# RWKV's odd heads run in the same rounds as the even heads instead of five rounds behind

## The reference

```python
def wkv7_scan(r, w, k, v, a, bb):
    def step(S, inp):
        r_t, w_t, k_t, v_t, a_t, b_t = inp
        sa = jnp.einsum('bhvk,bhk->bhv', S, a_t)
        S = S * w_t[:, :, None, :] + sa[..., None] * b_t[:, :, None, :] + v_t[..., None] * k_t[:, :, None, :]
        return S, jnp.einsum('bhvk,bhk->bhv', S, r_t)
...
    y = wkv7_scan(rh, decay.reshape(b, s, H, N), kh, vh, -kk, kk * ah)
```

## Time and profile before

| | |
|---|---|
| median of 3 runs | 3024.86 us (3021.54 to 3025.31) |
| span of the profiled execution | 3025.1 us; the page gives no other time of its own |
| PE busy | 2901.6 us, 96% |
| DVE busy | 2112.8 us, 70% |
| ACT busy | 1564.3 us, 52% |
| POOL busy | 680.0 us, 22% |
| rounds in which heads run | 1283 to 1883 us of the span |

### The profile page before, as it was taken

One profiled execution on the slowest core, in us unless ns is written; L12 is line 12 of the kernel. 1 busy time (PEld: TensorE's weight loads), 2 busy tenths in 40 slices (PEclk: granted clock), 3 DMA queues, 4 the chain that ended last, 5 costly groups with the idle time before them and its releaser, 6 DMA issues.

```text
span 3025.1 us, 52413 instructions
## 1 busy us (share of the span) xinstructions
PE 2901.6 (96%) x21006; PEld 2597.7 (86%) x21006; DVE 2112.8 (70%) x3455; ACT 1564.3 (52%) x2611; POOL 680.0 (22%) x869
## 2 busy tenths in 40 slices
PE   8977999999999999899899999998999999999998
PEld 8867998888888888888788888997888888888887
DVE  7888877865778656677777776777666665566654
ACT  6445555543555545366555555555445444444443
POOL 0455311210111000565455540001000110011100
PEclk9888999999999999899999999999999999999999
DMA  6312555556555555322222223454555555655554
GB/s 255 130 42 94 172 176 188 194 170 194 206 184 193 167 176 207 112 99 95 88 92 92 92 92 113 153 182 152 176 173 183 193 190 171 209 188 189 186 173 143
DMA packets 79825, 475.34 MB, mean 157 GB/s; under 512 B 8224, under 2 KB 11296, under 8 KB 38304
## 3 DMA queue, kind: packets, MB, share of 16 engines
q1 hardware_dynamic: 76768, 459.66, 44.3%
q10 hardware_dynamic: 2816, 12.32, 1.2%
HBM read 465.66 MB, written 6.29 MB: 156 GB/s over the span
## 4 chain that ended last, share of the span: by engine, by line
PE 77%; DVE 10%; issue 6%; ACT 4%; POOL 2%; DMA 0%; SPq 0%; ACTq 0%; POOLq 0%; DVEq 0%
PE bank L720 33%; PE bank L724 22%; PE bank L722 6%; PE bank L723 5%; DVE m L1247 2%; PE bank L742 1%; ACT m L2177 1%; POOL m L2901 1%; PE bank L1046 1%; POOL m L2897 1%; DVE m L1572 1%; PE bank L1050 1%; PE bank L1157 0%; PE bank L1008 0%; PE bank L1015 0%
## 5 line engine op out<-in xcount | busy, mean ns | idle before, releaser
L724 PE MATMUL bank<-m,m 128*128 128x256 f32 x6864 | 1930.3, 281 | 0.0
L720 PE MATMUL bank<-m,m 128*128 128x512 f32 x4736 | 1657.1, 394 | 5.7 <-DVE m L2051 5.7
L1247 DVE TENSOR_TENSOR m<-m,m 128x1024 fp32r<-128x1024 f32 (+1 forms) x944 | 1072.5, 1144 | 613.2 <-ACT m L2177 606.9
L724 PEld LDWEIGHTS bank<-m,m 128*128 128x128 f32 x6864 | 1300.3, 189 | 0.9
L2177 ACT ACTIVATE m<-m 128x1024 fp32r<-128x1024 f32 (+1 forms) x944 | 911.6, 979 | 712.9 <-PE bank L724 689.2
L720 PEld LDWEIGHTS bank<-m,m 128*128 128x128 f32 x4736 | 890.8, 188 | 203.4 <-DVE m L2051 5.9
L722 PE MATMUL bank<-m,m 128*128 128x256 f32 x2128 | 637.3, 299 | 29.2 <-DVE m L1247 23.5
L723 PE MATMUL bank<-m,m 128*128 128x256 f32 x2128 | 604.7, 284 | 0.0
L722 PEld LDWEIGHTS bank<-m,m 128*128 128x128 f32 x2128 | 409.7, 193 | 53.5 <-issue 42.9
L723 PEld LDWEIGHTS bank<-m,m 128*128 128x128 f32 x2128 | 410.2, 193 | 1.9
L2877 POOL TENSOR_TENSOR m<-m,m 128x256 fp32r<-128x256 f32 x44 | 63.4, 1441 | 683.0 <-ACT m L2454 683.0
(11 more groups left out here) (382 smaller groups left out, 2892.4 us busy)
## 6 DMA issues: line engine op xcount, KB each, us to landing
m<-in_w_up SPq DMA_DIRECT2D x88, 1024.0 KB, 4.8
m<-in_w_down SPq DMA_DIRECT2D x128, 704.0 KB, 4.1
m<-in_w_gu SPq DMA_DIRECT2D x88, 1024.0 KB, 4.8
m<-in_w_out SPq DMA_DIRECT2D x48, 1024.0 KB, 5.1
m<-in_w_krv SPq DMA_DIRECT2D x48, 1024.0 KB, 4.8
m<-in_w_xbc SPq DMA_DIRECT2D x24, 1024.0 KB, 4.8
m<-in_w_z SPq DMA_DIRECT2D x16, 1024.0 KB, 4.8
m<-in_w_in SPq DMA_DIRECT2D x14, 1024.0 KB, 6.6
```

The lines of the kernel that those rows point to most:

```text
L720: pe.matmul(bank.rearrange("p (a b) -> p a b", a=2), hi, x, start=kc == L.k0, stop=False)
L724: m = pe.matmul(ps, lo, x[:, 0, :], start=False, stop=last)
L1247: v.tensor_tensor(lo_of(k), raw_of(k)[0], hi_of(k).bitcast(F32), SUB).then_inc(*lo_v(("lo", k)))
```

## The change

The odd heads' generator starts each pair in the same round as the even heads', not five rounds later. `tails` and `afters` keep their rounds, and no instruction is added or removed.

```diff
     def heads(e):
-        return timed(*((PAIRS + ROUNDS * b + 5 * e, chain(block(2 * b + e, 0), block(2 * b + e, 1))) for b in range(8)))
+        return timed(*((PAIRS + ROUNDS * b, chain(block(2 * b + e, 0), block(2 * b + e, 1))) for b in range(8)))
 
     tails = timed(*((PAIRS + ROUNDS * (i // 2 + 1) + 5 * (i % 2), tail(i)) for i in range(16)))
```

## The result

The changed kernel takes 3046.51 us, the median of 4 runs (3043.06 to 3049.17), against 3023.92 (3021.54 to 3025.31) for the kernel before on the same chip. The ratio is 1.0073, with a 95% interval of 1.006 to 1.0085: slower, as forecast, inside the range, but by 22.6 us instead of 32. The profiled spans give the same picture, 3043.9 against 3025.1 us, so 18.8 us more.

What follows compares the result with a forecast made beforehand. PE, busy 96% of the span, was taken as the bound, losing time where it waits. Steady cycles at 5.9 us gave 23.6, plus 5.3 and 3: 32 us on 3025.1, so 3057 us, range 3034 to 3074.

Steps and rivals of the forecast that it cites:

- What bounds it: PE, busy 96% of the span, loses time where it waits; ACT sets the end in rounds 9 to 13.
- What is free: No instruction added or removed; odd heads ending five rounds sooner saves nothing, as PE does those matmuls either way.
- Rounds 0 to 7 free for waits: No prep there; ACT's spreads and DVE's two L1879 are wanted later, so costed at nothing.
- Round 8: L950 waits for L1931 behind a second state copy, 0.75 us instead of 0.2: +0.55 a cycle.
- Rounds 9 to 13: ACT 2.5 us late at the weight cut, so L1015 waits 3.0 us for L1879 instead of 1.05: +1.95 a cycle.
- Cycle 0: Like a steady cycle but without tails: 5.9 - 0.55 = 5.3 us slower.
- Round 11: ACT 0.55 us late from two more copies, so PE waits at L1001 for L2547: +0.5 a cycle.
- The clock: One fall to 1.2 GHz a cycle, after L1015's wait of 3.0 us, lasting 6.8 us: +3.1 a cycle.
- Rounds 15 to 17: DVE some 3 us late: waits of 1.6 us in rounds 16 and 17 at full clock, none with a fall.
- Cycles 2, 6, 7: Cycle 2: +3 us, bounds 0 and 5.9; cycles 6 and 7: taken as 0, between -2 and +6.
- The rival "faster": In step, waits at L1046 in rounds 6 to 9 and 16 to 19 go: -10 us, 3015; chance 0.09.

Runs made afterwards that it cites:

- experiments 2: Changed kernel with ACT's spreads L2553 late, even head's at end of step 2, odd head's at end of step 3: 3030.06 us, ratio 1.0019 to the kernel before.
- experiment 5: Changed kernel with both heads' spreads late (ends of steps 2 and 3) and the odd tail one round earlier: 3026.65 us, ratio 1.0012 to the kernel before.
- experiment 9: Changed kernel with only the odd head's spread L2553 late, at the end of its step 3: 3036.05 us, ratio 1.0037 to the kernel before.
- experiment 1: Changed kernel, but on PE alone the odd head's step stands two steps of main behind the even head's: 3084.88 us, ratio 1.0201 to the kernel before.
- experiment 4: Changed kernel with the odd head's tail one round earlier: 3034.48 us, ratio 1.0037 to the kernel before.
- experiment 8: Changed kernel, late spreads everywhere, early odd tail for pairs 0 to 5, pairs 6 and 7 five rounds apart: 3025.01 us, ratio 1.0000 to the kernel before.
- experiment 7: Changed kernel with the odd heads one round behind the even heads, tails unchanged: 3034.03 us, ratio 1.0037 to the kernel before.
- experiment 3: Kernel before, odd heads still five rounds behind, with both heads' spreads late (ends of steps 2 and 3): 3026.15 us, ratio 1.0002 to the kernel before.

## Why the prediction was right in direction and too high

The account of cycle 4, from the windows: PE's idle time is 75.40 - 70.72 = 4.7 us against 1.5, **+3.2**; the fall costs **+1.4**; PE's own work is 70.72 - 1.4 = 69.3 against 71.77, **-2.4**. Sum +2.2, and 75.40 - 73.24 is 2.2. The forecast had +5.9.

- **What bounds it.** Right: time was lost where PE waits, and at the engine named, ACT, in rounds 9 to 13.
- **"What is free": "those matmuls are PE's either way". This is the step that failed.** The matmuls are the same and their cost isn't. In step, like stands beside like and PE changes form 16 times fewer in a cycle. Own work fell by 2.4 us in cycle 4, and by 1.9, 2.0 and 2.1 in experiments 2, 5 and 9, at full clock: 15 to 19 us over eight cycles, 0.12 to 0.15 us a change. The pages agree: PE's busy time fell by 8.1 us although the mean granted clock fell from 0.981 to 0.977, some 25 us more at the lower level; at the 0.41 us of cost for each us there (1.4 for 3.4) that is 10 us, so its own work fell by some 18 (an estimate). With that term the forecast of 32 us would have been 13 to 17, against 18.8 measured. That form is the cause rests on experiment 1: the split costs time only in rounds whose form differs from `main`'s. The Trainium skill has the rule ("TensorEngine Tiling (Array Packing)", Key Properties): changing the tiling mode drains the engine, which changing the tile alone doesn't. The trace agrees as to the cost, 0.12 to 0.18 us a change; the drain itself no run here shows. I had read the change only for what waits, not for what stands beside what on PE.
- **Rounds 0 to 7 free for waits.** Right: in cycles 1, 3, 4 and 5 the trace shows no wait of PE there.
- **Round 8.** L950's wait was put at 0.75 and is 0.84. Experiment 4 gained 11.4 us by moving the tail, of which L950's waits are 6.6; the rest came with fewer falls of the clock, and that the one caused the other isn't shown.
- **Rounds 9 to 13.** ACT's lateness was put at 2.5 us: L2177 starts 13.83 us after round 9 now and 11.70 before, 2.1. The missing 0.4 is a misreading of mine: ACT's work before was not one long run. It had a wait for DVE in it, in the part that the earlier trace rows leave out, and took up 0.43 us of its lateness there, as that wait is now 1.04 us and was 1.47. L1015's wait was put at 3.0 and is 3.36 to 3.46 in cycles 1, 3, 4 and 5. Both within 0.5 us, and experiment 9 confirms the chain nearly microsecond for microsecond (1.72 us out of ACT's run, 1.62 off the wait). Cycle 0, for which I had the same wait, has none, and had none before: the five waits in the earlier trace rows are those of cycles 1 to 5. ACT's wait inside its run, in the timeline of the kernel before:

```profile
1621.74 0.51 ACT L2470 ACTIVATE m<-m,m 128x256 f32<-128x256 f32 x1 [1.47 <-DVE m L1712]
```

- **Round 11.** The wait of 0.5 at L1001 didn't come in cycle 4. L2547 was to be 0.55 us late; it starts 6.53 us after round 9 now and 6.33 before, 0.2 later, as ACT's wait for DVE took up the rest here too.
- **The clock.** The fall came, in all four cycles, and was mis-sized: I had 6.8 us at the low level and 3.1 us of cost each. It was 6.8 long in cycles 1 and 5 and 3.4 in 3 and 4. The cost in cycle 4 is 1.4; in cycle 5 it is 2.9 (PE busy 72.13 us, and 69.26 in the cycle 5 of experiment 4, which has no fall). (Cycle 7 had a longer wait at L1001, 2.95 us for 1.91, and a longer low stretch than the earlier trace rows.) I had taken the length from one fall, in cycle 7. The price for each us at the low level was nearly right, 0.46 by the earlier trace rows and 0.41 to 0.42 measured, though what stands in it is L1015 and L932 and not `main` alone.
- **Rounds 15 to 17.** Right: with a fall 0.30 us is left; without, in experiment 9, 2.1 (forecast 1.6).
- **Cycles 2, 6, 7.** I had +3 for cycle 2 and it is +3.3; 0 for cycles 6 and 7, and they are +1.1 and, with all that follows, +2.1. Cycle 0 was put at 5.3 and is 1.8. That cycles 6 and 7 are near 0 is luck: PE's idle time grew by 3.3 us in cycle 6 (5.3 against 2.0) and by 4.9 from cycle 7 on (31.5 against 26.6), where L1001 waits 2.95 us for 1.91 and L1071 of the last tails 3.50 for 0.41, and PE's cheaper work paid for most of it.

Added up, the forecast had 13.5 us of new waits in cycles 0, 1, 3, 4 and 5, 15.5 of falls and 3 for cycle 2. Measured are 26.9 us of idle time, some 10 of falls and 18 less of PE's own work. So the time is inside the range partly by luck: waits that I didn't see and a saving that I didn't see stand against each other.

The rival "faster" had a true half, which its text didn't name. Its place, L1046 for L1900, was wrong: those waits went up, from 5.1 us to 8.3. But order does save PE time, by form, and had ACT had the 2.5 us free, the change would have been near even: experiment 5 has steady cycles of 72.4 us against 73.2.

What stays open: why the clock falls behind some waits and not behind others, and so why it fell less in experiment 4 and elsewhere in experiment 8; what would spare cycles 0 and 6 their longer waits in step. That no version was faster is shown only for those tried.

## What to carry to other kernels

When two like streams of work are put in step, follow the engine with the longest run of in-order work ahead of something that a third engine needs (here ACT's weight cut), and add to it all that both streams now issue in that run: this came out within 0.5 us. Look for waits inside the run, which take up part of what is added (0.4 us here). Then read the bound engine itself: count how often its neighbours in the order change form, before and after, since the same matmuls in another order don't cost the same. Take the cost of a fall of the clock from the matmuls that will stand in it, and its length from more than one fall.

## What the runs showed of the hardware that I had not expected

- PE pays for a change between matmuls of different weight form: about 0.18 us each by experiment 1 (4.9 us for 28), 0.2 by experiment 7 (1.5 us for 7), 0.12 to 0.15 by the comparison with before (1.9 to 2.4 us for 16). Round 9 of experiment 1 by itself gives 0.17. Between steps of the same form as `main` nothing was seen (2.76 and 2.75 us).
- The clock's fall behind a wait isn't certain by the wait's length alone. It stayed at 1.00 behind 1.74 us in experiment 9 and 3.45 in cycle 5 of experiment 4, and it fell behind 3.36 here, behind 1.91 in the earlier trace rows and behind 1.75 in cycle 6 of experiment 3. In experiment 1 the same wait of 2.9 us comes in cycles 1, 3, 4 and 5; the clock fell in 3 and 5 and stayed up in 1 and 4. The low stretches lasted 3.4, 6.8 or, in cycle 7 after the change, 10.2 us.
- The first matmul behind a wait takes longer at full clock too, but only by 0.10 us. In experiment 9 the two heads' L1015 take 1.18 us behind the wait of 1.74, and 0.81 in round 3 of the changed kernel. The single records of the trace split the difference: the first takes 0.378 us where the others take 0.275; the odd head's first takes 0.372, as its own L1879 ended only 0.06 us before it; and L932, of another form, starts 0.21 us behind the last one, where L722 starts 0.03 behind it in round 3.
